# Block one's norms: first products on unscaled rows with the row factor applied behind them, splits and table loads moved, wide head sums

## The reference, cut to what matters

```python
for l in range(2):
    h = rms_norm(x, norm_mix[l]); z = h @ w_in[l]          # 2560 columns
    mix = concat(attention(z), hgrn2(z), conformer_conv(z))
    x = x + mix @ w_out[l]
    h = rms_norm(x, norm_mlp[l])
    x = x + square(relu(h @ w_mlp_in[l])) @ w_mlp_out[l]   # 4096 wide
```

## Time and profile before

| what | value |
|---|---|
| median of 3 runs | 3776.9 us (3773.65 to 3781.3) |
| the profiled execution's own time | 3782.67 us |
| its span | 3780.9 us |
| TensorE busy | 3603.8 us, 95% |
| VectorE busy | 2106.8 us, 56% |
| ScalarE busy | 1398.6 us, 37% |
| GpSimd busy | 869.3 us, 23%, all in the first 2150 us or so |
| mean granted TensorE clock | 0.985 |
| chain that ended last | TensorE 77%, VectorE 16%, ScalarE 4% |

### The profile page before, as it was taken

How to read it: one execution, slowest core, us unless ns; L and a number is a source line. 1 busy time by engine, 2 the same in 40 slices (tenths; PEclk the granted TensorE clock), 3 DMA queues, 4 the chain that set the end, 5 groups by cost and what they waited for, 6 DMA issues and landing times.

```text
span 3780.9 us, 47130 instructions
## 1 busy us (share of the span) xinstructions
PE 3603.8 (95%) x18583; PEld 2904.8 (77%) x18583; DVE 2106.8 (56%) x2762; ACT 1398.6 (37%) x1873; POOL 869.3 (23%) x716
## 2 busy tenths in 40 slices
PE   7989999998999999999899999999989999989998
PEld 5667888766788878887567888788868778777887
DVE  5967444596743454347666444633574655665434
ACT  4664332366432332223663212222233434332223
POOL 3210655321065536552213640000000000000000
PEclk9999999999999999999899999999999999999999
DMA  6212655421265556663224643233322222223331
GB/s 162 64 44 67 152 142 143 106 75 44 66 154 138 150 117 150 146 153 70 61 68 101 161 127 91 81 98 100 101 76 76 73 76 87 63 66 89 100 90 67
DMA packets 564437, 377.56 MB, mean 100 GB/s; under 512 B 37489, under 2 KB 561354, under 8 KB 564218
## 3 DMA queue, kind: packets, MB, share of 16 engines
q1 hardware_dynamic: 564218, 374.56, 37.6%
HBM read 372.32 MB, written 2.17 MB: 99 GB/s over the span
## 4 chain that ended last, share of the span: by engine, by line
PE 77%; DVE 16%; ACT 4%; issue 2%; SPq 0%; DMA 0%; DVEq 0%; ACTq 0%
PE bank L446 62%; DVE conv_sum L1290 2%; PE bank L454 2%; DVE w_lo L424 2%; PE bank L492 2%; PE bank L893 1%; PE bank L486 1%; ACT w_hi L415 1%; PE bank L487 1%; DVE std L955 1%; DVE norm_tmp L1749 1%; DVE norm_tmp L1743 1%; DVE X L1745 1%; DVE dil_probs L2542 1%; PE bank L2376 1%
## 5 line engine op out<-in xcount | busy, mean ns | idle before, releaser
L446 PE MATMUL bank<-H_hi,w_hi 128*128 128x512 f32 x2384 | 958.3, 402 | 5.4 <-DVE w_lo L424 1.8
L446 PE MATMUL bank<-H_hi,w_lo 128*128 128x512 f32 x2384 | 932.9, 391 | 0.0
L446 PE MATMUL bank<-H_lo,w_hi 128*128 128x512 f32 x2384 | 932.1, 391 | 0.0
L424 DVE TENSOR_TENSOR w_lo<-w_raw,w_hi 128x2048 fp32r<-128x2048 f32 (+3 forms) x285 | 654.6, 2297 | 147.7 <-ACT w_hi L415 139.5
L415 ACT ACTIVATE w_hi<-w_raw 128x2048 fp32r<-128x2048 f32 (+3 forms) x285 | 529.1, 1857 | 307.5 <-DMA w_raw<-in_ffn_w_up 129.3
L446 PEld LDWEIGHTS bank<-H_hi,w_hi 128*128 128x128 f32 x2384 | 448.8, 188 | 131.3 <-issue 38.4
L525 POOL TENSOR_TENSOR w_mod_raw<-w_mod_raw,silu_c 128x1024 f32<-128x1024 f32 x144 | 280.3, 1946 | 1169.5 <-DMA w_mod_raw<-in_w_mod 1123.6
L446 PE MATMUL bank<-U_hi,w_hi 128*128 128x512 f32 x1376 | 539.5, 392 | 3.8 <-DVE note L1012 3.8
L446 PE MATMUL bank<-U_hi,w_lo 128*128 128x512 f32 x1376 | 535.9, 389 | 0.0
L446 PE MATMUL bank<-U_lo,w_hi 128*128 128x512 f32 x1376 | 535.6, 389 | 0.0
L446 PEld LDWEIGHTS bank<-H_hi,w_lo 128*128 128x128 f32 x2384 | 448.7, 188 | 96.6 <-issue 0.3
(11 more groups left out here) (370 smaller groups left out, 4632.5 us busy)
## 6 DMA issues: line engine op xcount, KB each, us to landing
w_mod_raw<-in_w_mod SPq DMA_DIRECT2D x576, 128.0 KB, 5.8
w_raw<-in_ffn_w_gate SPq DMA_DIRECT2D x88, 512.0 KB, 4.0
w_raw<-in_ffn_w_up SPq DMA_DIRECT2D x88, 512.0 KB, 5.4
w_raw<-in_dil_w_in SPq DMA_DIRECT2D x36, 1024.0 KB, 5.1
w_raw<-in_w_mlp_in SPq DMA_DIRECT2D x32, 1024.0 KB, 6.0
w_raw<-in_w_mlp_out SPq DMA_DIRECT2D x32, 1024.0 KB, 5.8
w_raw<-in_ffn_w_down SPq DMA_DIRECT2D x32, 1024.0 KB, 5.4
w_raw<-in_w_in SPq DMA_DIRECT2D x16, 1024.0 KB, 5.6
```

Of the source, the lines that this page charges most:

```text
L424: dve.eng.tensor_tensor(WL[u % SLOTS][:, 0:n], RAW[u % SLOTS][:, 0:n], WH[u % SLOTS][:, 0:n].bitcast(F32), ALU.subtract).then_inc(lo_done. ...
L446: mm = pe.eng.matmul(bank[0:m, :], w[:, k, c0:c0 + m], r[:, k, :], start=(k == 0 and i == 0), stop=(k == kt - 1 and i == 2))
```

## The change

In block one, VectorE and ScalarE make the high and low halves of x times the feature gain, without the token's factor. `pe_raw_pair` takes the place of `pe_pair`: the stage's first two units are multiplied with these halves, while the sums, root and spread run at chosen places inside the pair. Only then are the scaled halves made, into the same tiles, for the third unit onward; the pair's results are multiplied by the factor in bank 5 afterwards (`z_scaled` for z, `scale_mid` behind relu for `up`). The third unit of each such stage waits for scaled tiles one by one. Its split stands ahead of the root. In layer 0 the pair is done in two sets of two tiles; x is loaded to another place, the parameter tables 0 and 1 are loaded from ScalarE's queue, and tables 2 and 3, the fixed matrices and the bias tables by SyncE behind the first two weight units; their products stand inside the pair. The silu for the modulation comes behind the root, followed by a load of the root's table. The lower-bound operations move to points 54 and 58 of the mixer. The head sums write 32 equal columns per head, in three banks, so the root becomes three instructions. In the diff below the indentation is cut by one level, and the engines' waits for their own last instruction are left out.

```diff
+    units[lin[("z", l)][0]]["waits"] = "tiles"
...
-        add_units(("up", l, q), H, [square(w1, D_FF, 1024 * q + 256 * i) for i in range(4)], "none" if q else "tiles")
+        add_units(("up", l, q), H, [square(w1, D_FF, 1024 * q + 256 * i) for i in range(4)], "none")
+        if q == 0:
+            units[lin[("up", l, q)][2]]["waits"] = "tiles"
...
-XS = at("x_rows", h_at, [P, NB, D])
+XS = at("x_rows", y_at, [P, NB, D])
...
+def pe_raw_pair(pe, u, at_pass, apart=False):
+    rh, rl = H
+    todo = []
+    for v in (u, u + 1):
+        n = units[v]["cols"]
+        wh, wl = (W[v % SLOTS][:, 0:DT * n].rearrange("p (k n) -> p k n", n=n) for W in (WH, WL))
+        for j, (_, c0, m, _) in enumerate(units[v]["tiles"]):
+            todo.append((wh[:, :, c0:c0 + m], wl[:, :, c0:c0 + m]) + acc_place[units[v]["tiles_at"] + j])
+    sets = [todo[0:2], todo[2:4]] if apart else [todo]
+    for s, together in enumerate(sets):
+        pe.eng.wait_ge(lo_done.sem, u + (s + 1 if apart else 2))
+        for k in range(DT):
+            if s == 0:
+                pe.eng.wait_ge(raw_hi.sem, raw_hi.next(pe))
+            for wh, wl, place, turn in together:
+                if k == 0:
+                    pe.eng.wait_ge(acc_free[place].sem, turn - 1)
+                pe.eng.matmul(banks[place][:], wh[:, k], rh[:, k, :], start=(k == 0), stop=False)
+                pe.eng.matmul(banks[place][:], wl[:, k], rh[:, k, :], start=False, stop=False)
+            if s == 0:
+                pe.eng.wait_ge(raw_lo.sem, raw_lo.next(pe))
+            for wh, wl, place, turn in together:
+                mm = pe.eng.matmul(banks[place][:], wh[:, k], rl[:, k, :], start=False, stop=(k == DT - 1))
+                if k == DT - 1:
+                    mm.then_inc(acc_ready.sem, acc_ready.add())
+            if k < DT - 1 and s == len(sets) - 1:
+                mm.then_inc(raw_used.sem, raw_used.add())
+            for job in at_pass.get((s, k), ()):
+                job(pe)
+    part_hi.taken["pe"] = part_hi.taken.get("pe", 0) + DT
...
+def mixh_squares(act, l):
+    u, gain = lin[("mixh", l)][0], lambda t: colp("norm_mlp", 8 * l + t)
+    def high(t):
+        place, turn = acc_place[units[u]["tiles_at"] + t]
+        act.eng.wait_ge(acc_free[place].sem, turn)
+        raw_high(act, t, gain)
+    def square_of(t):
+        if t >= 2:
+            act.eng.wait_ge(sq_summed.sem, sq_summed.next(act, 0 if t == 3 else 1))
+        act.eng.activation(SQ[t % 2][:], X[:, t, :], ACT.Square).then_inc(sq_run.sem, sq_run.add())
+    act.eng.activation(NOTE[:, 1:2], NOTE[:, 1:2], ACT.Sqrt).then_inc(act.step.sem, act.step.add())
+    act.eng.wait_ge(act.step.sem, act.step.made)
+    for t in range(4):
+        high(t)
+    square_of(0)
+    square_of(1)
+    for t in range(4, DT):
+        high(t)
+    split_hi(act, lin[("up", l, 0)][2])
+    for t in range(2, DT):
+        square_of(t)
+    sq_summed.taken["act"] += 1
...
+def raw_high(act, t, gain):
+    act.eng.activation(H[0][:, t, :], X[:, t, :], ACT.Identity, scale=gain(t)).then_inc(raw_hi.sem, raw_hi.add())
+def raw_low(dve, t, gain):
+    dve.eng.wait_ge(raw_hi.sem, raw_hi.next(dve))
+    dve.eng.scalar_tensor_tensor(H[1][:, t, :], X[:, t, :], gain(t), H[0][:, t, :].bitcast(F32), ALU.mult, ALU.subtract).then_inc(raw_lo.sem, raw_lo.add())
+def scaled_high(act, u, ahead_of):
+    for t in range(DT):
+        for job in ahead_of.get(t, ()):
+            job()
+        act.eng.wait_ge(scaled.sem, scaled.next(act))
+        if t < DT - 1:
+            act.eng.wait_ge(raw_used.sem, raw_used.next(act))
+        else:
+            act.eng.wait_ge(acc_ready.sem, units[u + 1]["tiles_end"])
+        act.eng.activation(H[0][:, t, :], NT[2 + t % 2][:], ACT.Identity).then_inc(part_hi.sem, part_hi.add())
+def scaled_tiles(dve, gain, ahead_of):
+    ve = dve.eng
+    dve.eng.wait_ge(rbc_ready.sem, rbc_ready.next(dve))
+    for t in range(DT + 1):
+        if t < DT:
+            ve.scalar_tensor_tensor(NT[2 + t % 2][:], X[:, t, :], gain(t), banks[5][:], ALU.mult, ALU.mult).then_inc(scaled.sem, scaled.add())
+        for job in ahead_of.get(t, ()):
+            job()
+        if t:
+            dve.eng.wait_ge(part_hi.sem, part_hi.next(dve))
+            ve.tensor_tensor(H[1][:, t - 1, :], NT[2 + (t - 1) % 2][:], H[0][:, t - 1, :].bitcast(F32), ALU.subtract).then_inc(rhs_ready.sem, rhs_ready.add())
+def rstd_column(dve):
+    dve.eng.wait_ge(std_ready.sem, std_ready.next(dve))
+    dve.eng.reciprocal(RSTD[:, 0:NB], STD[:, 0:NB]).then_inc(rstd_ready.sem, rstd_ready.add())
...
+        if gain and t:
+            raw_low(dve, t - 1, gain)
+        if gain and t == DT - 1:
+            raw_low(dve, t, gain)
...
 def last_mix(dve, l):
-    u = lin[("mixh", l)][0]
+    u, gain = lin[("mixh", l)][0], lambda t: colp("norm_mlp", 8 * l + t)
+    split_lo(dve, u + AHEAD)
     for t in range(DT):
         bank, free = acc_take(dve, u, t)
         dve.eng.tensor_tensor(X[:, t, :], X[:, t, :], bank[:], ALU.add).then_inc(free.sem, free.add())
         dve.eng.wait_ge(free.sem, free.made)
-        if t >= 2:
-            add_squares(dve, t - 1)
-    split_lo(dve, u + AHEAD)
+        if t in (4, 5):
+            raw_low(dve, t - 4, gain)
+    for t in range(2, DT):
+        raw_low(dve, t, gain)
+        add_squares(dve, t - 1)
+    split_lo(dve, lin[("up", l, 0)][2])
+    rstd_column(dve)
...
+def scale_mid(dve, u, j):
+    place, turn = acc_place[units[u]["tiles_at"] + j]
+    dve.eng.wait_ge(acc_free[place].sem, turn)
+    dve.eng.tensor_tensor(MID[j][:], MID[j][:], banks[5][:], ALU.mult).then_inc(high_scaled.sem, high_scaled.add())
...
+        if q == 0 and u - lin[("up", l, 0)][0] < 2:
+            if u != lin[("up", l, 0)][0]:
+                for j in range(2):
+                    relu_into_mid(act, u, j)
+            for j in range(2):
+                act.eng.wait_ge(high_scaled.sem, high_scaled.next(act))
+                act.eng.wait_ge(mid_used.sem, mid_used.next(act, lag=2))
+                act.eng.activation(MID[2 + j][:], MID[j][:], ACT.Square).then_inc(square_r.sem, square_r.add())
+            return
...
+        if q == 0 and n == 1:
+            for j in range(2):
+                scale_mid(dve, u, j)
+            dve_note(dve, rbc_used)
...
+    put(54, ("bound", 0))
+    put(58, ("bound", 1))
...
+HEAD_SUM_BANK = (4, 6, 5)
...
-            mm = te.matmul(banks[4][:, 8 * i + 2 * b:8 * i + 2 * b + 2], HEAD_SQ[i][:, b * P:(b + 1) * P], PAIR[:, 0:2], start=True, stop=True)
+            c0 = 256 * (i % 2) + 64 * b
+            mm = te.matmul(banks[HEAD_SUM_BANK[i // 2]][:, c0:c0 + 64].rearrange("p (h c) -> p h c", c=32), HEAD_SQ[i][:, b * P:(b + 1) * P],
+                           PAIR[:, 0:2].unsqueeze(2).to_broadcast([P, 2, 32]), start=True, stop=True)
...
-    pe_pair(pe, lin[("z0", l)][0])
+    if l == 0:
+        jobs = {(0, 5): [bias_products], (0, DT - 1): [after_bias, pe_running_sums], (1, 0): [pe_spread]}
+    else:
+        jobs = {(0, 0): [pe_running_sums], (0, 1): [pe_spread]}
+    pe_raw_pair(pe, lin[("z0", l)][0], jobs, l == 0)
...
-        ae.activation(QSTD[:], banks[4][:, 0:40], ACT.Sqrt, bias=EPSC[:], scale=1.0 / HEAD).then_inc(qk_std.sem, qk_std.add())
-        act.eng.wait_ge(qk_std.sem, qk_std.made)
+        for n, (bank, w) in enumerate(zip(HEAD_SUM_BANK, (16, 16, 8))):
+            total = banks[bank][:, 0:32 * w].rearrange("p (x h c) -> p x h c", h=2, c=32)[:, :, :, 0]
+            signal = qk_std if n == 2 else act.step
+            ae.activation(QSTD[:, 16 * n:16 * n + w].rearrange("p (x h) -> p x h", h=2), total, ACT.Sqrt, bias=EPSC[:],
+                          scale=1.0 / HEAD).then_inc(signal.sem, signal.add())
...
+def z_scaled(dve, u, j, slot):
+    place, turn = acc_place[units[u]["tiles_at"] + j]
+    dve.eng.wait_ge(acc_free[place].sem, turn)
+    dve.eng.tensor_tensor(Z[:, slot, :], Z[:, slot, :], banks[5][:], ALU.mult).then_inc(high_scaled.sem, high_scaled.add())
...
-        z_evac(act, first + t // 2, t % 2, t)
-    for t in range(4):
+        act.eng.wait_ge(high_scaled.sem, high_scaled.next(act))
         head_square(act, t)
...
+def bias_products(pe):
+    pe.eng.wait_ge(fixed_in.sem, fixed_in.next(pe, 16))
+    pe.eng.wait_ge(bias_tab_in.sem, bias_tab_in.next(pe, 48))
+    turn_params(pe, (2, 3))
...
+    for t in range(2):
+        raw_high(act, t, lambda t: colp("norm_mix", t))
+    split_hi(act, 0)
+    for t in range(2, 4):
+        raw_high(act, t, lambda t: colp("norm_mix", t))
+        square_of(t - 2)
+    split_hi(act, 1)
+    for t in range(4, DT):
+        raw_high(act, t, lambda t: colp("norm_mix", t))
+        square_of(t - 2)
+    for t in range(DT - 2, DT):
+        square_of(t)
     sq_summed.taken["act"] += 1
...
+def modulation_act(act):
+    act.eng.wait_ge(rstd_ready.sem, 1)
+    act.eng.activation(CSIL[:], colp("c_2", 0, 32), ACT.Silu).then_inc(csil_ready.sem, csil_ready.add())
...
+    take_params(dve, (0, 1))
+    for t in range(2):
```

(68 more changed lines are left out.)

118 lines of the change are left out of this document (77 added, 41 removed).

## The result

The changed kernel takes 3782.48 us (median of 20 runs, 3776.4 to 3786.73), the kernel before 3778.22 beside it (20 runs). The ratio is 1.0014, 95% interval 1.0007 to 1.0020: 4.3 us slower. That lies within the 0.2% called no change, though the interval leaves out equal times. Forecast were 3773.9 us and a range up to 3782. The profiled execution took 3785.07 us.

The account below looks back on a forecast made before the run. TensorE sets the pace nearly everywhere, VectorE from 97 to 201 us. Parts 1.5 + 0.6 + 2.2 + 2.0 - 2.8 - 0.5 = 3.0 us gained: 3779.7 us profiled, 3773.9 us as median; range 3761 to 3782.

Parts of the forecast that it names:

- Part 1: `up` of layer 0: third unit 28.0 us in against 32.93, 4.9 gained, less 3.4 of wait: 1.5 us gained.
- Part 2: `up` of layer 1: same working against 32.03 us, 4.0 less 3.4: 0.6 us gained.
- Part 3: `z` of layer 1: next stage at 720.9 us against 723.23, 2.2 us gained; bounds 0 and 3.4.
- Part 4: Head of layer 0: products start earlier, scaled chain limits, POOL's bursts take 2.0: 2.0 us gained; bounds -2 and 6.
- Part 5: Lower-bound operations moved into the layer-0 mixer, in VectorE's full queue: 2.8 us lost; range 0 to 4.4.
- Part 6: Wide head sums, ten groups at 0.05 us each: 0.5 us lost; range 0 to 1.3.
- The rule that I weighed: Head: each low part in POOL's window could wait a full POOL instruction of 1.90 us, making 5 us, not 2.
- Rival (b): Head, `up`, mixer, z: two-operand VectorE operations wait for whole POOL instructions; 13.6 us slower at full price, 3786 at two thirds; chance 0.08.
- Rival (a): Head, `up`, mixer: delays covered throughout, 13 to 18 us gained, 3761 us; chance 0.30.
- all three debts: Waits before `up`'s fourth unit in layers 0 and 1, 3.4 us each, and the bounds in the mixer, 2.8.
- (c): Products are not brought forward, raw parts late and the pair waits as before: 3777 to 3780 us; with the forecast 0.62.

Follow-up runs that it names:

- POOL cut: POOL's modulation operations cut to 8 columns or fewer in both kernels: 3752.33 us for the kernel before, 3745.17 us for the changed kernel.
- the fillers: Changed kernel with 26 filler products of 256 columns in the first z unit of layer 0: 3778.29 us, 1.0001 of before.
- the late silu: Changed kernel with the modulation's silu and its two table loads moved from ahead of the scaled chain to behind the fourth copy of z: 3776.02 us.
- Three moves: Changed kernel with silu and loads behind z's fourth copy, bounds at points 112 and 120, `up`'s fourth split ahead of second unit's casts: 3769.79 us.
- fourth split early: Changed kernel with the split of `up`'s fourth unit moved ahead of the second unit's casts, both layers: 3779.45 us, 1.0006 of before.
- relu first: Changed kernel with the first relu of `up`'s pair moved ahead of the seventh scaled high part, both layers: 3788.24 us, 1.0025 of before.

## Why the prediction was wrong

The sum said 3.0 us gained; in the profiled execution block one lost 3.0. The steps that failed are the head (2.0 gained forecast, 0.5 lost) and the bounds (2.8 lost forecast, 4.3 lost), and a term that is in no part: TensorE's clock, which the sum put at nothing.

- **Part 1, right.** From the pair's first product (339.55 us) to the third unit 28.2 us, forecast 28.0, before 32.93. It waits 2.43 us for the relu, forecast 2.7. The fourth unit starts 13.9 us behind the third, 3.0 more than its 48 products need, forecast 3.4; but 1.1 is the wait, and 1.7 the clock's lower level from 369.1 to 372.5, so the size is right in part by luck. POOL's burst began at 373.51 us, on the casts as named. Measured over the whole: 1.5 us gained, forecast 1.5.
- **Part 2, right.** 28.4 us to the third unit, forecast 28.0; the whole 0.8 us, forecast 0.6.
- **Part 3, right.** The pair begins at 700.45 us, 1.2 us behind the last down product as forecast, and the third unit at 725.14. From the start of that last product it is 26.3 us, before 28.7 (694.50 to 723.23): 2.4 gained, forecast 2.2.
- **Part 4, wrong, the first step that failed.** Products at 20.19 us (forecast 20.5), table loads at 38.48, first high part 42.8 and its end 43.45 (forecast 43.8), POOL at 40.09 (40.4), the pair's end 49.0 (49.5): all as told. But the last low part ended at 61.4 instead of 59.5. I had priced "two bursts up to 3.0, I take 2.0"; POOL had four tiles to work on and lengthened the eight low parts by 4.4 us together, shown by the same chain without it. That alone leaves the eighth row tile where it was before (61.42 against 61.46), and the forecast gain of 2.0 is gone. What I did not price at all is the clock behind it, where the prediction has only "stops at its eighth row tile until 57.5": TensorE passes that tile at half the clock, until 65.3 us, which cost 1.8 us here and 3.5 to 5.4 in three others of the same head. Not all of it shows against before, which has 1.2 us in the same stretch that its twin without POOL's work does not have. The profiled execution lost 0.5 in the head, the other three lost 4.0, 4.2 and 6.6 (up to 2.5 of it by a later start of the chain).
- **Part 5, mis-sized and its mechanism wrong.** 2.8 forecast, 4.3 measured. It was counted as VectorE's time in a full queue. The runs show that by itself it is nothing: with POOL cut, the offset over that stretch stays as it was. With POOL the cast took 0.65 us instead of 0.23 and the exponent, which I had put in no queue, waited 3.35 us on ScalarE ahead of the attention.
- **Part 6, mis-sized.** 0.5 forecast, 0 measured.

Two losses are in no part, 0.9 us between 78 and 106 us and 1.8 in layer 1's recurrence, and the traces point to the clock for both. From 93 to 112 us the changed kernel is low for 6.8 us, before for 3.4; of the kernels that leave the silu in its place, those with 3.4 us low lose nothing there (−0.2 to 0.0 us), and the one other with 6.8 loses 1.0. In the recurrence (860 to 960 us) the changed kernel is low for 10.2 us, before for 6.8. Between the splits at 853 and 974 us the three variants with 6.8 us low lose 0.4 us, the changed kernel and the fillers with 10.2 lose 1.6, four with 13.7 lose 1.6 to 3.9, and two with 20.5 lose 4.2 and 4.7.

**The rule that I weighed.** The Trainium skill (SBUF — State Buffer, "Who interferes with whom") has a VectorE instruction with two SBUF inputs contend with a GpSimd instruction that reads SBUF, for ports that one of them locks while the other waits. In the head the low parts took 0.85 to 2.02 us beside POOL's 1.90, 1.62 and 1.29, so two of eight waited 1.3 us, two 0.5 to 0.6 and four 0.2: neither every operation at full price nor one in eight. The two longest started 0.42 us behind a POOL instruction of 1.90 us and ended 0.5 us behind its end, as if they had waited for it. The 4.4 us in all lie near the 5 that I gave this rule, not at the 2 that I took; but eight operations at 1.90 us each would be 15, so that the 5 comes near is luck. Rival (b), which stood on it, had the right sign and, with 13.6 us at full price and 9 at two thirds, the wrong size: `up` and z did as forecast. Rival (a) is refuted: all three debts came. So is (c): the head's products came 11.5 us sooner.

**Why the change doesn't bring its gross gain**, then: against the late silu 4.5 us of the head are lost to the scaled chain, stretched by POOL, and 1.8 or more to the clock behind it, 4.3 to the bounds, some 3 of the two `up` to the fourth unit's split. Three moves give most of it back, and that kernel is faster than both, by 0.23% against before.

## What to carry over

When work is brought forward, ask which chain sets the next unit's last tile, and what will run beside that chain in its new place. Don't put the release of a neighbour's work (here the silu, for POOL) just ahead of a chain whose operations lengthen beside it; released behind the chain it cost less, though not nothing: 2.4 of 5.1 us were gone 28 us later. A low TensorE clock is worth what is low behind the last wait, about half of its length, and nothing where a later wait covers it: so price not only the waits in the middle of a unit but also the clock behind them. And a wait that is shortened is worth something only if the next instruction's own supplier isn't already late: of the two waits in `up` the second was the one to remove.

## What was not expected of the hardware

- Kernels wait about as long in the head and differ in the clock: 2.15 us (silu late) without a fall, 1.88 and 0.73 us between 52.0 and 55.6 us (changed kernel) with one; with POOL's work cut waits of 0.9 and 0.6 us had one behind them. Once low, it mostly stayed so for 10 to 24 us while short waits went on; with fillers it rose after 3.4 us, and once (fourth split early) after 3.4 us without any, to fall again 3.4 us later.
- The same code with the same data differs from one execution to the next: the kernels with all of POOL's work spread over 6.6 to 16 us, and with POOL's bursts cut over 3 to 4, though in 4 and 5 executions only. That the clock makes this spread is likely, but not shown: only one execution of each kernel has a trace.
- Not only operations with two SBUF operands lengthen beside POOL, as I had read from the rows of before: a cast of 128x512 took 1.98 instead of 0.43 us (relu first, 377.49 us), one of 128x128 0.65 instead of 0.23. VectorE, relu first:

```profile
377.49 1.98 DVE L1010 CAST U_hi<-mid 128x512 fp32r<-128x512 f32 x1
379.50 1.65 DVE L1012 TENSOR_TENSOR U_lo<-mid,U_hi 128x512 fp32r<-128x512 f32 x1
```
